# Swish straight from PSUM, and lists, bias rows and divisions reordered, in a mixture-of-experts layer

## The reference

```python
gu = lax.ragged_dot(xs, w_gu, group_sizes) + b_gu[e_sorted]
g, u = gu[:, :EXPERT_FF], gu[:, EXPERT_FF:]
g = jnp.minimum(g, SWIGLU_LIMIT)                       # 7.0
u = jnp.clip(u, -SWIGLU_LIMIT, SWIGLU_LIMIT)
act = (u + 1) * (g * jax.nn.sigmoid(SWIGLU_ALPHA * g)) # 1.702
out = lax.ragged_dot(act, w_down, group_sizes) + b_down[e_sorted]
```

## Time and profile before

| | us |
|---|---|
| median of 3 runs | 2721.61 (2721.31 to 2721.8) |
| profiled execution, its own time | 2723.34 |
| its span, first to last instruction | 2721.7 |
| expert stage, 1012 to 2665 | 1653.00 |

### The profile page before, as it was taken

One profiled execution on the slowest core, in us unless ns is written; L12 is line 12 of the kernel. 1 busy time (PEld: TensorE's weight loads), 2 busy tenths in 40 slices (PEclk: granted clock), 3 DMA queues, 4 the chain that ended last, 5 costly groups with the idle time before them and its releaser, 6 DMA issues. The chain is left out here.

```text
span 2721.7 us, 55797 instructions
## 1 busy us (share of the span) xinstructions
PE 2425.6 (89%) x19101; PEld 1359.0 (50%) x19102; DVE 1597.6 (59%) x1872; ACT 1347.3 (50%) x1395; POOL 817.0 (30%) x860
## 2 busy tenths in 40 slices
PE   6999978799999938889899999789998999999992
PEld 2545543667765524445455554345554455554550
DVE  1121226566645545881772777998679725166875
ACT  1111125256542225781762667888668725165871
POOL 1122212330002334432332443335343323233332
PEclk9999988899999959999999999899999999999996
DMA  8000015250012245992781878999889926167975
GB/s 303 28 17 17 9 62 206 71 138 0 0 71 110 93 173 194 339 389 50 274 336 36 294 265 294 402 397 395 295 290 398 332 80 216 31 223 278 335 270 203
DMA packets 180310, 538.46 MB, mean 198 GB/s; under 512 B 20736, under 2 KB 37554, under 8 KB 180206
## 3 DMA queue, kind: packets, MB, share of 16 engines
q1 hardware_dynamic: 150620, 487.79, 47.2%
q0 software_dynamic: 26720, 46.85, 7.9%
q10 hardware_dynamic: 2916, 3.14, 0.3%
HBM read 493.11 MB, written 45.20 MB: 198 GB/s over the span
## 5 line engine op out<-in xcount | busy, mean ns | idle before, releaser
L1955 PE MATMUL psum<-arena 128*64 128x512 bf16 x12528 | 1425.2, 383 | 67.4 <-DVE arena L1859 44.4
L1955 PEld LDWEIGHTS psum<-arena 128*64 128x64 bf16 x12528 | 725.0, 111 | 718.1 <-DVE arena L1859 52.0
L1855 DVE TENSOR_TENSOR arena<-arena 128x2048 bf16<-128x2048 f32 x384 | 862.8, 2287 | 173.6 <-ACT arena L1775 162.8
L1775 ACT ACTIVATE arena<-arena 128x2048 bf16<-128x2048 f32 x384 | 721.9, 1902 | 97.8 <-DVE arena L1855 70.6
L1727 POOL DMA_INDIRECT expert_sums<-arena x90 | 169.5, 1884 | 475.9 <-issue 461.7
L537 PE MATMUL psum<-arena 128*128 128x512 f32 (+2 forms) x864 | 303.9, 509 | 1.1 <-ACT arena L394 1.1
L1707 POOL DMA_INDIRECT arena<-expert_inputs,arena x88 | 130.7, 1485 | 537.8 <-DMA arena<-expert_lists 515.0
L537 PEld LDWEIGHTS psum<-arena 128*128 128x128 f32 x864 | 151.6, 192 | 131.8 <-issue 127.0
L1859 DVE TENSOR_TENSOR arena<-psum,arena 128x512 bf16<-128x512 f32 x87 | 60.0, 690 | 252.9 <-ACT arena L1785 252.9
L1796 ACT ACTIVATE arena<-psum,arena 128x512 f32<-128x512 f32 x87 | 59.4, 683 | 209.9 <-PE psum L1955 140.4
L1738 POOL DMA_DIRECT2D arena<-expert_lists x174 | 128.8, 925 | 29.0 <-issue 24.5
(11 more groups left out here) (253 smaller groups left out, 2258.0 us busy)
## 6 DMA issues: line engine op xcount, KB each, us to landing
arena<-in_w_gu SPq DMA_DIRECT2D x256, 1024.0 KB, 18.8
arena<-in_w_down SPq DMA_DIRECT2D x128, 1024.0 KB
arena<-in_w_ada SPq DMA_DIRECT2D x12, 2048.0 KB, 9.0
arena<-in_x_sample SPq DMA_DIRECT2D x16, 512.0 KB, 3.2
arena<-in_w_in SPq DMA_DIRECT2D x3, 2048.0 KB, 19.1
expert_sums<-arena SPq DMA_DIRECT2D x10, 512.0 KB, 6.4
expert_inputs<-arena SPq DMA_DIRECT2D x10, 512.0 KB, 2.8
x_after_mixing<-arena SPq DMA_DIRECT2D x9, 512.0 KB, 2.7
```

The source lines that it names most:

```text
L1775: nc.scalar.activation(w_hi[p][c], raw[p][c], ACT.Copy).then_inc(sem(f"hi_made{c}"), 1)
L1855: nc.vector.tensor_tensor(w_lo[p][c], raw[p][c], w_hi[p][c], ALU.subtract).then_inc(sem(f"lo_made{c}"), 1)
L1955: last = nc.tensor.matmul(bank(b)[group(g)], parts[part][:, cols], w[:, kk, g * H:(g + 1) * H], start=False, stop=(k == KT - 1 and part == 1))
```

## The change

1. `gate` is gone. `sigmoid` reads the gate product from PSUM, `swish` multiplies PSUM by the sigmoid, and the minimum is taken of the Swish value (`SWISH_TOP`, the value at 7) in the last step of `up`. The up bias has 1 added on GpSimd in an earlier stage, and the clip's bounds become 8 and -6. `g_made`, for which TensorE's next gate bias waits, is now set by `swish`.
2. GpSimd copies the unit's list to `present`, gathers with it, and right behind the gather requests the list of the next unit (`fetch`); the first list is requested ahead of the loop.
3. ScalarE requests the next expert's bias rows right behind the last unit's sigmoid, once the up product's first chunk is done (`used4`), and no more behind `keep_x`.
4. In the last unit of an expert with several, ScalarE makes one division ahead of `act_hi`, not two.
5. First stage: the square of the context tile is computed ahead of those ten requests; these wait for the second piece of `w_ada`; VectorE waits for three shift copies ahead of the addition, not for four ahead of the norm; GpSimd waits for the small tables later.

```diff
@@ -262,6 +263,7 @@
         tstart = kept(NE + 1).bitcast(I32)
         tlast = kept(NE).bitcast(I32)
         listed, held, moved = kept(2).bitcast(I32), kept(2 * DELAY + 2), kept(2 * DELAY)
+        present = kept(2).bitcast(I32)
         assert to[0] <= W
...
@@ -343,6 +345,9 @@
                 act.dma_start(xs[0], x_ctx).then_inc(sem("x_in0"), 16)
                 act.wait_ge(sem("condT_made"), 1)
                 nc.scalar.activation(sgc, bank(7, 2 * KT), ACT.Sigmoid).then_inc(sem("cond_sig"), 1)
+                act.wait_ge(sem("x_in0"), 16)
+                nc.scalar.activation(xjunk, xs[0], ACT.Square, accum_out=ss).then_inc(sem("x_squared"), 1)
+                act.wait_ge(sem("ada1_parted"), 2)
                 act.dma_start(xs[1], x_lat[0:P, :]).then_inc(sem("x_in1"), 16)
                 act.dma_start(rope[1], t_in["rope"][0:P, :]).then_inc(sem("rope_in1"), 16)
                 act.dma_start(nw[:, 0:HD], spread(t_in["q_norm"][0])).then_inc(sem("norms_in"), 16)
@@ -353,8 +358,6 @@
                 act.dma_start(expert, spread(t_in["expert_id"])).then_inc(sem("norms_in"), 16)
                 act.dma_start(pickrow.bitcast(I32), t_in["bias_rows"]).then_inc(sem("norms_in"), 16)
                 act.dma_start(brt, spread(t_in["b_router"][0])).then_inc(sem("norms_in"), 16)
-                act.wait_ge(sem("x_in0"), 16)
-                nc.scalar.activation(xjunk, xs[0], ACT.Square, accum_out=ss).then_inc(sem("x_squared"), 1)
                 for i in range(2, 4):
                     for k, mods in enumerate((mAc, mA)):
                         act.wait_ge(sem("mod1_summed"), 2 * i + k + 1)
@@ -403,7 +406,6 @@
                 nc.gpsimd.memset(pickedsum, 0.0).then_inc(sem("const_set"), 1)
                 pool.wait_ge(sem("ident_in"), 16)
                 nc.gpsimd.tensor_copy(identb, ident).then_inc(sem("const_set"), 1)
-                pool.wait_ge(sem("norms_in"), 16 * 8)
                 pool.wait_ge(sem("const_set"), 4)
                 def norm_x(n):
@@ -418,6 +420,7 @@
                 pool.wait_ge(sem("x_normed"), 1)
                 nc.gpsimd.memset(lrT1[2 * RANK:LR1, :], 1.0).then_inc(sem("gate_w_cleared"), 1)
                 pool.wait_ge(sem("gate_w_cleared"), 3)
+                pool.wait_ge(sem("norms_in"), 16 * 8)
...
@@ -474,7 +477,6 @@
                 scale_keep(1)
                 part_keep(3)
                 dve.wait_ge(sem("scale_kept"), 4)
-                dve.wait_ge(sem("shift_kept"), 4)
...
@@ -482,6 +484,8 @@
                     nc.vector.tensor_scalar(msq, ss, 1.0 / DM, EPS, ALU.mult, ALU.add).then_inc(sem("x_mean"), 1)
                     wait(dve, sem("x_rstd"), g + 1)
                     own.link(nc.vector.scalar_tensor_tensor(xs[slot], xs[slot], rstd, mods[0], ALU.mult, ALU.mult))
+                    if isinstance(g, int):
+                        dve.wait_ge(sem("shift_kept"), 3 + g)
                     nc.vector.tensor_tensor(xs[slot], xs[slot], mods[1], ALU.add).then_inc(sem("x_normed"), 1)
...
@@ -1056,6 +1060,9 @@
                 q_slices(1, None)
                 for k, n in enumerate((2 * FF, FF)):
                     pool.wait_ge(sem("braw_in"), 16 * k + 16)
+                    if k == 0:
+                        nc.gpsimd.tensor_scalar(braw[:, FF:2 * FF], braw[:, FF:2 * FF], 1.0, None, ALU.add).then_inc(sem("up_bias_raised"), 1)
+                        pool.wait_ge(sem("up_bias_raised"), 1)
                     for i in range(3):
                         if i:
                             pool.wait_ge(sem("bias_rest"), 2 * k + i)
...
@@ -1646,6 +1653,7 @@
         opening = lambda j: isinstance(j, int)
         group = lambda g: slice(64 * g, 64 * g + 64)
         B_GATE, B_UP, B_Y, B_ACT, B_X = range(5)
+        SWISH_TOP = 7.0 / (1.0 + math.exp(-1.702 * 7.0))
...
@@ -1705,7 +1713,7 @@
                     wait(pool, sem("x_turned"), j + 1)
                     settle(pool, "pool_steps")
                     pool.indirect_dma_start(out=xg, out_offset=None, in_=h2_d,
-                                            in_offset=bass.IndirectOffsetOnAxis(ap=listed.bitcast(U32)[:, 0:1], axis=0)).then_inc(sem("gathered"), 16)
+                                            in_offset=bass.IndirectOffsetOnAxis(ap=present.bitcast(U32)[:, 0:1], axis=0)).then_inc(sem("gathered"), 16)
...
                     wait(pool, sem("moved_made"), j + 1)
                     settle(pool, "pool_steps")
                     if fresh:
-                        nc.gpsimd.tensor_copy(held[:, 0:2], listed.bitcast(F32)).then_inc(sem("taken"), 1)
+                        nc.gpsimd.tensor_copy(held[:, 0:2], present.bitcast(F32)).then_inc(sem("taken"), 1)
                     else:
                         pool.sem_inc(sem("taken"), 1)
                     nc.gpsimd.tensor_copy(held[:, 2:2 * DELAY + 2], moved).then_inc(sem("taken"), 1)
...
-                def body(e, j, s):
-                    wait(pool, sem("gathered"), j * 16)
-                    wait(pool, sem("taken"), j * 2)
-                    row = nc.s_assert_within(e * LISTW + (j - s) * UNIT, 0, (NE - 1) * LISTW + TOK - UNIT,
+                def fetch(e, at):
+                    row = nc.s_assert_within(e * LISTW + at * UNIT, 0, (NE - 1) * LISTW + TOK - UNIT,
                                              skip_runtime_bounds_check_because="an expert has at most TOK rows, in TOK / 64 units")
                     pairs = list_d[ds(row, UNIT), :].rearrange("t (h w) -> t h w", h=2)
                     for h in range(2):
                         pool.dma_start(listed[group(h), :], pairs[:, h, :]).then_inc(sem("listed_in"), 16)
+
+                def body(j, following):
+
                     wait(pool, sem("listed_in"), j * 32 + 32)
+                    if not opening(j):
+                        wait(pool, sem("gathered"), j * 16)
+                        wait(pool, sem("taken"), j * 2)
+                    settle(pool, "pool_steps")
+                    nc.gpsimd.tensor_copy(present, listed).then_inc(sem("present_kept"), 1)
+                    wait(pool, sem("present_kept"), j + 1)
                     gather(j)
+                    if following is not None:
+                        fetch(*following)
                     shift(j, True)
                     add_up(j)
-                with pool.Fori(0, NE) as e:
-                    s, n = bound(pool, e), bound(pool, e + 1)
-                    with pool.Fori(s, n) as j:
-                        body(e, j, s)
+                def units(e):
+                    s, last = bound(pool, e), last_unit(pool, e)
+                    with pool.If_lt(pool.to_reg(s), last):
+                        with pool.Fori(s, last) as j:
+                            body(j, (e, j + 1 - s))
+                    body(last, None if final(e) else (e + 1, 0))
+
+                fetch(0, 0)
+                with pool.Fori(0, NE - 1) as e:
+                    units(e)
+                units(NE - 1)
                 T = pool.value_load(tstart[0:1, NE:NE + 1], min_val=0, max_val=MAX_UNITS)
                 wait(pool, sem("gathered"), T * 16)
...
@@ -1785,10 +1809,10 @@
                     nc.scalar.activation(aT_hi, bank(B_ACT), ACT.Copy).then_inc(sem("ahi_made"), 1)
                 def sigmoid(j):
-                    wait(act, sem("g_made"), j + 1)
+                    wait(act, sem("used3"), j + 1)
                     if not opening(j):
                         wait(act, sem("act_turned"), j)
-                    nc.scalar.activation(uact, gsig, ACT.Sigmoid, scale=1.702).then_inc(sem("sig_made"), 1)
+                    nc.scalar.activation(uact, bank(B_GATE), ACT.Sigmoid, scale=1.702).then_inc(sem("sig_made"), 1)
                 def result(j):
                     wait(act, sem("used11"), j + 1)
@@ -1813,10 +1837,13 @@
                             hi(*at)
                     if last:
-                        divide(2)
+                        divide(2 if first else 1)
                     if not opening(j):
                         act_hi(j - 1)
                     sigmoid(j)
+                    if last:
+                        wait(act, sem("used4"), n)
+                        bias_gu(e + 1)
                     divide(2)
                     if opening(j):
                         act.wait_ge(sem("x_turned"), 3)
@@ -1824,8 +1851,6 @@
                         nc.scalar.activation(xT, bank(B_X).bitcast(BF), ACT.Copy).then_inc(sem("xT_made"), 1)
                     else:
                         keep_x(j + 1)
-                    if last:
-                        bias_gu(e + 1)
                     divide(2 if first else 1)
                     if not opening(j):
                         result(j - 1)
@@ -1858,20 +1883,16 @@
                     wait(dve, sem("ahi_made"), j + 1)
                     nc.vector.tensor_tensor(aT_lo, bank(B_ACT), aT_hi, ALU.subtract).then_inc(sem("alo_made"), 1)
-                def gate(j):
-                    wait(dve, sem("used3"), j + 1)
```

(12 more changed lines are left out.)

## The result

The changed kernel takes 2745.9 us (median of four runs, 2738.2 to 2752.3), the kernel before, on the same chip, 2721.7 (2721.3 to 2725.0): ratio 1.0085, interval 1.0058 to 1.0112. It is slower by 0.85%; 2676.5 was predicted, in a range of 2654 to 2705, and faster at 0.93. The profiled execution is the quickest of the four (2738.2 us).

A forecast was written before the change was run, and what follows sets the result against it. TensorE was taken to set the pace, held up by act_lo, bias rows and divided chunks. Gains 3.1 + 8 + 34 = 45.1 took 2723.3 to 2678.2, less 1.7 for the median: 2676.5 us, range 2654 to 2705.

The forecast's parts named there:

- One division ahead: Last units of several: act_hi one division (2.2 us) sooner, VectorE's second division up to 2.9 us later, but hidden.
- Rival 3: ScalarE's wait for the up product's first chunk starves VectorE in all 31 last units: slower, 2767 us; chance 0.04.
- first stage: Before the experts: context tile's norm runs beside the last products, 3.1 us sooner on TensorE's path, between 0 and 5.
- start of the expert stage: First units: lists requested sooner, second transposes' 5.56 us wait goes, some given back at gate bias; 8 us, bounds 4 and 11.
- 1098:1207: Crowded stretch, experts of 2, 1, 2 units: earlier result, VectorE's lead and the last bias wait give 8 us.
- 1311:1394: Crowded stretch with one single-unit expert: no lead, 0.8 us gained plus its last bias wait of 2.25; 3 us.
- 1657:1860: Crowded stretch, three single-unit experts among pairs: 2.3 us and two bias waits of 2.3 and 2.0; 6.5 us.
- 1860:2002: Stretch of two-unit experts: two bias waits and the slower matmuls behind them go; 4.5 us.
- 2002:2140: Two single-unit experts with a pair between: 0.5 + 0.7, and 2.5 from a result that waited for shift; 3.5 us.
- rest of the stage: Expert stage outside the five listed stretches: 6 us in 2540:2665 (pairs), 0 at the single-unit expert outside them.
- small waits: TensorE's small waits for bias rows elsewhere, outside the listed stretches, end: 2.5 us.
- Rival 1: VectorE and DMA take it back: near single-unit experts bias waits become chunk waits; total 28 us, 2694; chance 0.22.

The follow-up runs named there:

- trimmed kernel: Changed kernel without the redundant wait for act_turned ahead of ScalarE's sigmoid, loop at 625 to 954: 2685.5 us, ratio 0.9862 to the kernel before.
- padded by 90: Changed kernel with 90 idle instructions on ScalarE, executed once ahead of the loop, which moves to 717 to 1054: 2689.6 us, ratio 0.9887 to the kernel before.
- first stage undone: Changed kernel without the redundant sigmoid wait, its first stage put back as before the change: 2688.8 us, ratio 0.9884 to the kernel before.
- rows undone: Changed kernel without the redundant sigmoid wait, bias-row request and division order (parts 3 and 4) put back: 2694.0 us, ratio 0.9902 to the kernel before.

## Why the prediction was wrong, step by step

**The failed step** is one that the prediction doesn't have. Under "One division ahead" it prices what the new `wait(act, sem("used4"), n)` adds by when the wait ends and what queues behind it: a request of 0.3 us, a high part of 1.9. It does not count the instructions: a net one more in each of the loop's four `last` bodies takes the loop from 334 to 338 instructions, and the first body ahead of the loop moves it on by one. That passed an edge which the kernel before missed by a single instruction. It costs 0.0223 of 2721.6 us against the trimmed loop and 0.0198 against the padded one, 54 to 61 us, and turned a gain into a loss. The prediction took ScalarE's instructions as there when their turn comes, and so had no term for fetching them. The edge shows on no row of the kernel before except by what isn't there, packets on q14 between 1140 and 2620 us. Rival 3 has the sign right, but its mechanism (VectorE starved by the wait) isn't what happened. The whole expert stage of the changed and of the trimmed kernel:

```profile
1000.20:2683.30 1683.10, 1563.45 (x14102) 823.13 (x14102) 1072.24 (x728) 1015.95 (x791) 599.14 (x695) 0.97 0.74 264
...
1006.50:2628.00 1621.50, 1541.87 (x14102) 818.78 (x14102) 1071.25 (x728) 1016.94 (x791) 601.00 (x695) 0.99 0.76 274
```

TensorE stands still for 119.6 us instead of 79.6 (length less busy time), and its matmuls take 21.6 us longer at the lower granted clock.

**The sum.** With the loop in place the change gives 2689.6 us as written (padded by 90) and 2685.5 trimmed, 9 to 13 above the 2676.5 predicted and inside its range. The trimmed kernel's windows over the same units:

```profile
1087.78:1186.41 98.63, 90.11 (x812) 47.77 (x810) 92.19 (x57) 86.79 (x62) 40.58 (x40) 0.97 0.99 370
1290.47:1372.15 81.68, 71.62 (x650) 37.79 (x648) 73.31 (x45) 70.09 (x50) 34.68 (x32) 1.00 0.98 363
1632.72:1828.45 195.73, 166.76 (x1460) 84.64 (x1458) 178.54 (x107) 170.26 (x119) 74.77 (x72) 0.97 1.01 384
1828.45:1967.96 139.51, 139.47 (x1298) 75.82 (x1296) 105.15 (x71) 97.60 (x75) 54.31 (x65) 1.00 0.92 339
1967.96:2095.12 127.16, 111.05 (x974) 56.00 (x972) 115.41 (x70) 111.08 (x79) 51.36 (x47) 0.97 1.00 377
2095.12:2608.60 513.48, 505.55 (x4700) 271.28 (x4698) 285.06 (x210) 270.54 (x225) 178.97 (x227) 1.00 0.63 217
```

| term | predicted | measured |
|---|---|---|
| first stage | 3.1 | 6.0, give or take 6 (first stage undone) |
| start of the expert stage | 8 | 5.0 |
| 1098:1207 | 8 | 20.5 - 12.1 = 8.4 |
| 1311:1394 | 3 | 15.0 - 12.4 = 2.6 |
| 1657:1860 | 6.5 | 43.1 - 40.1 = 3.0 |
| 1860:2002 | 4.5 | 7.0 - 1.1 = 5.9 |
| 2002:2140 | 3.5 | 26.1 - 23.3 = 2.8 |
| rest of the stage | 6, and a part of the 2.5 for small waits | 20.6 - 12.5 = 8.1 |

*First stage.* In the changed kernel its addition (L489) is done in time for the transposes to start at 38.05 us; 40.3 was predicted. The other 2.3 us are the weights: the last product with `w_ada` ahead of them starts at 31.18 instead of 33.44, which the prediction has under its upper bound of 5. The expert stage's first transposes start at 1010.8 to 1014.4 us in the six profiles with the old first stage and at 1000.3 to 1010.6 in the ten with the new one, 5 us sooner in the mean, so most of it lasts.

*Start.* The second transposes now wait 0.87 us instead of 5.56:

```profile
1010.09 0.62 PE L1953 MATMUL psum<-arena 128*128 128x128 bf16 x8 [0.87 <-DMA arena<-expert_inputs,arena]
...
1018.18 0.41 PE L1964 MATMUL psum<-arena 128*64 128x512 bf16 x2 [1.96 <-issue]
```

The gate bias behind them waits, as said, but for 1.96 us, and the product behind it for 2.9 more; from GpSimd's first memset to the fourth unit's transposes it is 70.0 us before and 65.1 after, so 5 where 8 was taken and 4 the lower bound.

*Bias rows, list, swish.* Two of the five stretches come within 0.5 us, two more within 1.4, and 1657:1860 gives half of what was said; there VectorE is busy for 178.5 of 195.7 us. The waits that were to go are gone. But the prices behind the sum are not those of the parts: bias rows and divisions are worth 10.9 us where some 21 were put on them, the swish 27.8 where it was some 5. That the sum fits so well is in part luck. Wrong was to price the swish and the division order separately; on the kernel before, the swish alone brings 13.1, and with the swish as before the other part is a loss.

Rival 1's mechanism is there, too. With the rows undone TensorE waits for bias rows and for chunks

```profile
PE psum L1972 <- DVE arena L1877: 16.4, 28, 1.1
PE psum L1961 <- DMA arena<-bias_parts: 12.0, 12, 1.8
```

28.4 us together, and in the trimmed kernel as long for chunks alone:

```profile
PE psum L1973 <- DVE arena L1878: 28.1, 41, 1.3
```

What the part brings is quicker matmuls. The whole expert stage with the rows undone:

```profile
1006.20:2637.00 1630.80, 1550.97 (x14102) 829.08 (x14102) 1072.29 (x728) 1020.52 (x791) 588.16 (x695) 0.98 0.76 272
```

TensorE stands still for 79.8 us, as long as in the trimmed kernel; its matmuls take 1551.0 instead of 1541.9 us, at a granted clock of 0.98 instead of 0.99.

*Waits.* For `act_lo` the prediction has about 35 us; the trimmed kernel, without pauses, has 39.5:

```profile
PE psum L1973 <- DVE arena L1882: 39.5, 15, 6.9
```

## What to carry to other kernels

Before a change that adds instructions or waits inside an engine's long loop, look at the instruction queues of the page: packets per pass of the loop say whether it stays in the engine. Count the loop in the compiled program and find its distance to the next edge; here one instruction executed once, ahead of the loop, cost 63 us, more than the change itself brings. When a kernel that should be quicker isn't, and an engine's wait is put down to "issue" right behind a loop's branch, move the loop before undoing the idea: padding and a dropped redundant wait each told it apart in one run.

## What the runs showed of the hardware

- A loop of 334 or 338 instructions on ScalarE repeats without a fetch (none on q14 between 1140 and 2620 us) when it touches three blocks of 128, and fetches five packets of 8.2 KB a pass when it touches four. Good were 624 to 949, 625 to 954, 626 to 959 and 717 to 1054; bad 627 to 960 through 659 to 996, and 757 to 1094. Where the count starts is this program's own, so the edges as numbers hold for it only. That room is kept for four blocks, one of them the block ahead, fits all runs and isn't shown otherwise.
- In the changed kernel ScalarE stands still for 5.2 to 5.7 us behind the loop's closing branch in each of the 14 returns (0.2 us in the trimmed one), and twice for 3.2 us behind another branch of the pass (L1632). About 81 us of pauses (63.3 + 17.8) cost 54 to 61.
- A pause costs what slack doesn't cover: 5.98 us of idle ScalarE ahead of 1384.04 left TensorE a wait of 0.90 (at 1386.71); in the expert of one unit shown above TensorE's gap grew by 4.6 us, and the granted clock of the fullest stretch (1657:1860 before) is 0.92, where it is 0.97 in the trimmed kernel. Of the 61.6 us between the two expert stages 40 are standing still and 21.6 slower matmuls.
- Not settled: whether dropping the redundant wait is worth something by itself (0.9862 against 0.9887, whose intervals overlap), and whether DMA load makes the fetch longer.
